# Gate and up products of two ffn stages by Strassen's method

## What is computed

```python
D_FF = 2816
hn = rms_norm_2(h, ffn_norm[l])
gu = hn @ w_gate_up[l]
h = h + (jax.nn.silu(gu[..., :D_FF]) * gu[..., D_FF:]) @ w_down[l]
```

## Time and profile before

| | us |
|---|---|
| median of 3 runs | 3443.02 |
| lowest, highest | 3441.24, 3450.82 |
| profiled execution | 3438.87 |
| its span (first to last instruction) | 3437.1 |
| TensorE matmuls busy (share of the span) | 3069.4 (89%) |
| VectorE busy | 1387.9 (40%) |
| ScalarE busy | 1115.5 (32%) |
| GpSimd busy | 250.7 (7%) |
| first layer: gate and up products | 2310.4 to 2552.2 |
| second layer: gate and up products | 3068.6 to 3310.2 |

### The profile page before, as it was taken

The page is one execution under the profiler, slowest core; times in us unless marked ns, Lnnn a source line. Parts: engine busy times, 40 slices in busy tenths (PEclk is TensorE's granted clock), DMA queues, the critical chain, the costliest instruction groups (busy, mean ns, idle before and its releaser), DMA issues. The chain is left out here.

```text
span 3437.1 us, 44411 instructions
## 1 busy us (share of the span) xinstructions
PE 3069.4 (89%) x17561; PEld 2178.1 (63%) x17561; DVE 1387.9 (40%) x2258; ACT 1115.5 (32%) x1938; POOL 250.7 (7%) x278
## 2 busy tenths in 40 slices
PE   7999999999698878887887698889999998889999
PEld 5777888878533333333333485868888775778887
DVE  6872566663430000000000467553332467553332
ACT  4672666762200000000000435432222336332222
POOL 0000332210000000000000000300000000300000
PEclk9999999999899999999999799999999998999999
DMA  5322222234699999999998520023333320023332
GB/s 135 89 76 80 74 68 68 74 91 136 251 379 429 429 429 429 430 429 429 429 429 357 157 74 13 6 93 98 96 95 104 94 57 1 20 92 96 98 98 92
DMA packets 361295, 612.37 MB, mean 178 GB/s; under 512 B 73952, under 2 KB 308224, under 8 KB 336384
## 3 DMA queue, kind: packets, MB, share of 16 engines
q1 hardware_dynamic: 351152, 598.72, 47.3%
q0 software_dynamic: 9216, 8.42, 0.7%
q10 hardware_dynamic: 720, 2.36, 0.2%
HBM read 605.23 MB, written 23.07 MB: 183 GB/s over the span
## 5 line engine op out<-in xcount | busy, mean ns | idle before, releaser
L268 ACT ACTIVATE f_hi<-f_raw 128x1024 fp32r<-128x1024 f32 x148 | 156.6, 1059 | 516.2 <-PE ff_bk L328 516.0
L1888 PE MATMUL ex_up<-ex_W,ex_XT 128*64 128x512 f32 x1024 | 249.9, 644 | 76.2 <-DMA ex_W<-in_w_expert_up_dram 76.2
L1888 PE MATMUL ex_gp<-ex_W,ex_XT 128*64 128x512 f32 x1024 | 241.3, 625 | 59.2 <-DMA ex_W<-in_w_expert_gate_dram 57.8
L326 PE MATMUL ff_bk<-h_b_hi,f_hi 128*128 128x512 f32 x704 | 276.1, 392 | 2.8 <-DVE h_b_lo L3860 2.8
L327 PE MATMUL ff_bk<-h_b_lo,f_hi 128*128 128x512 f32 x704 | 275.5, 391 | 0.0
L328 PE MATMUL ff_bk<-h_b_hi,f_lo 128*128 128x512 f32 x704 | 275.3, 391 | 0.0
L277 DVE TENSOR_TENSOR f_lo<-f_raw,f_hi 128x1024 fp32r<-128x1024 f32 x148 | 180.5, 1223 | 208.4 <-ACT f_hi L268 208.0
L1917 PE MATMUL ex_yp<-ex_W,ex_hT 128*64 128x512 f32 x1024 | 228.5, 598 | 34.3 <-DMA ex_W<-in_w_expert_down_dram 21.8
L1931 DVE TENSOR_TENSOR ex_hid<-ex_sg,ex_up 128x512 f32<-128x512 f32 x32 | 22.0, 688 | 580.7 <-PE ex_up L1888 580.7
L1888 PEld LDWEIGHTS ex_up<-ex_W,ex_XT 128*64 128x64 f32 x1024 | 89.6, 147 | 235.7 <-issue 235.7
L1888 PEld LDWEIGHTS ex_gp<-ex_W,ex_XT 128*64 128x64 f32 x1024 | 88.0, 144 | 211.3 <-issue 209.5
(11 more groups left out here) (612 smaller groups left out, 6305.8 us busy)
## 6 DMA issues: line engine op xcount, KB each, us to landing
ex_W<-in_w_expert_up_dram SPq DMA_DIRECT2D x64, 2048.0 KB, 37.6
ex_W<-in_w_expert_down_dram SPq DMA_DIRECT2D x64, 2048.0 KB, 38.4
ex_W<-in_w_expert_gate_dram SPq DMA_DIRECT2D x64, 2048.0 KB, 37.6
b_raw<-in_w_in_dram SPq DMA_DIRECT2D x88, 512.0 KB, 3.8
f_raw<-in_w_gate_up_dram SPq DMA_DIRECT2D x88, 512.0 KB, 3.7
f_raw<-in_w_down_dram SPq DMA_DIRECT2D x44, 512.0 KB, 3.5
m_raw<-in_w_in_dram SPq DMA_DIRECT2D x20, 512.0 KB, 4.1
m_early<-in_w_in_dram SPq DMA_DIRECT2D x20, 512.0 KB, 4.0
```

The source lines that it names most:

```text
L268: a.activation(self.hi[n % self.SLOTS][:, to], self.raw[n % self.RAW][:, at], ACT.Copy).then_inc(self.cast, 1)
L326: pe.matmul(out, a[0], b[0], start=first, stop=False)
L1888: ins = pe.matmul(ps[part[e], :], XT[b][:, q, part[e]], row_view(slots[e], KD)[:, q, :], start=(q == 0), stop=(q == KD - 1))
```

## The change

The gate and up products of a block are taken together as one product of a 2 x 2 matrix of halves. The contraction (1024) is halved into features 0 to 511 and 512 to 1023; the outputs are the gate half and the up half; the tokens are halved into 0 to 255 and 256 to 511. Strassen's method (in Winograd's form) makes seven products of half size where there were eight: 7 x 4 x 3 matmuls with 256 columns each, for 2 x 8 x 3 with 512.
- **The combinations of h.** Seven operands `hc[0..6]` (four tiles of 128x256 each, hi and lo). Two are quarters of h, one more is another quarter, four are sums of quarters. `make_sums` makes them from `xs` before they are transposed: three operations for token tiles 0 and 2 on GpSimd (s = 0), three for 1 and 3 on VectorE (s = 1). There are 14 groups of transposes, casts and low parts in place of 8, taken in between the products of block 0.
- **The combinations of weights.** `GateWeights` has nine slots of 128x512 (half a former tile), four raw buffers, and seven operands for each block u: three halves of the raw tiles and four sums, which GpSimd makes (`sum`, i = 3 to 6). ScalarE casts all seven to `hi`, VectorE makes all seven `lo`. A sum is written in the place where its `lo` will stand.
- **Putting together.** A block's results lie in four banks (blocks alternate between banks 0 to 3 and 4 to 7). ScalarE copies the first product (`keep_first`), VectorE makes `join_first` (128x512) and `join` (128x256, 128x512, 128x512), each with an operand in PSUM. Then ScalarE's silu, and on GpSimd the product with the up half (`gate_f`), into `raw_f`.
- **f is split later.** `raw_f` is held in float32; `make_f_hi` and `make_f_lo` stand in the down pass, two for each tile of down weights, in the order `FIRST_DOWN`.

The queues are again in order. VectorE's for pass u: low part 0 of block u + 1, join(u - 1), low parts 1 to 5, join_first(u), low part 6. ScalarE's: casts 0 and 1 of block u + 1, silu(u - 1), keep_first(u), casts 2 to 6. GpSimd's: sums 3 and 4 of block u + 1, gate_f(u - 1), sums 5 and 6. TensorE waits for join(u - 2) before block u.

```diff
+FIRST_DOWN = (3, 4, 5, 6, 7, 8, 9, 0, 1, 2, 10)
+F_ORDER = [2 * r + q for r in FIRST_DOWN for q in range(2)]
...
+class GateWeights:
+
+    SLOTS, RAW, EACH = 9, 4, 7
...
+    def wait_free(self, eng, w):
+
+        if w < self.SLOTS:
+            eng.wait_ge(self.W.used, 7 if w < 4 else 8)
+        else:
+            eng.wait_ge(self.used, w - self.SLOTS + 1)
...
+    def load(self, sp, g):
+
+        if g < self.RAW:
+            sp.wait_ge((None, self.W.split_done, self.W.split_done, self.W.used)[g], (0, 7, 8, 8)[g])
+        else:
+            self.wait_spent(sp, g - self.RAW)
+        dst = self.raw[g % self.RAW][:].rearrange("p (k n) -> p k n", n=P)
+        sp.dma_start(dst, self.tiles[g].rearrange("(k p) n -> p k n", p=P)).then_inc(self.loaded[g % self.RAW], 16)
...
+    def sum(self, p, u, i):
+
+        w = self.EACH * u + i
+        g1, g2, u1, u2 = self.halves(u)
+        raw = lambda j: self.sums[(self.EACH * u + j) % self.SLOTS]
+        self.wait_free(p, w)
+        if i == 3:
+            self.wait_loaded(p, 2 * u)
+            self.wait_loaded(p, 2 * u + 1)
+            p.tensor_tensor(raw(3), u1, u2, ALU.add).then_inc(self.summed, 1)
+        elif i == 4:
+            p.drain()
+            p.tensor_tensor(raw(4), raw(3), g1, ALU.subtract).then_inc(self.summed, 1)
+        elif i == 5:
+            p.drain()
+            p.tensor_tensor(raw(5), g2, raw(4), ALU.subtract).then_inc(self.summed, 1)
+        else:
+            p.tensor_tensor(raw(6), g1, u1, ALU.subtract).then_inc(self.summed, 1)
...
+    def make_lo(self, v, w):
+
+        u, i = divmod(w, self.EACH)
+        hi, lo = self.slot(w)
+        v.wait_ge(self.cast, w - 1)
+        if i in (3, 4):
+            v.wait_ge(self.summed, 4 * u + i - 1)
+        src = self.halves(u)[(0, 1, 3)[i]] if i < 3 else self.sums[w % self.SLOTS]
+        v.tensor_tensor(lo, src, hi.bitcast(F32), ALU.subtract).then_inc(self.split_done, 1)
...
+        def before_group(g):
+            if g < 4:
+                return xs[:, g // 2, (g % 2) * T:(g % 2 + 1) * T]
+            combo, s = g // 2, g % 2
+            if combo == 5:
+                return xs[:, 2 + s, T:]
+            lo = {2: 3 * T, 3: 0, 4: 2 * T, 6: T}[combo]
+            return sums[s][:, lo:lo + T]
...
+        def make_sums(eng, s):
+            x0, x1, out = xs[:, s, :], xs[:, 2 + s, :], sums[s]
+            taken = xs[:, s::2, 0:T]
+            eng.tensor_tensor(out[:, 0:2 * T].rearrange("p (a n) -> p a n", a=2), x1.rearrange("p (a n) -> p a n", a=2), taken, ALU.subtract)
+            eng.drain()
+            eng.tensor_tensor(out[:, 2 * T:3 * T], x1[:, T:], out[:, 0:T], ALU.subtract)
+            eng.drain()
+            eng.tensor_tensor(out[:, 3 * T:], x0[:, T:], out[:, 2 * T:3 * T], ALU.subtract).then_inc(sums_ready[s], 1)
...
-                for m in range(BLOCKS):
-                    for j in range(2):
-                        n = GU + 2 * m + j
-                        W.wait(pe, n)
-                        if m >= 2:
-                            pe.wait_ge((sig_ready, f_ready)[j], m - 1)
-                        for q in range(KD):
-                            ins = mm3(pe, bk[4 + 2 * j + m % 2][:], W.tile(n, q), both(h, q), q == 0, q == KD - 1)
-                        ins.then_inc(W.used, 1)
...
+                def gate_product(u, i):
+                    w = EACH * u + i
+                    bank, col = PLACE[i]
+                    out = bk[4 * (u % 2) + bank][:, col:col + 2 * P]
+                    hi, lo = G.slot(w)
+                    G.wait_split(pe, w)
+                    for q in range(4):
+                        at_q = slice(q * P, (q + 1) * P)
+                        ins = mm3(pe, out, (hi[:, at_q], lo[:, at_q]), both(hc[i], q), q == 0, q == 3)
+                    ins.then_inc(G.used, 1)
+
+                pe.wait_ge(x_added, 4)
+                for i in range(EACH):
+                    if i == 2:
+                        for g in range(4, 8):
+                            turn_middle(g)
+                    elif 3 <= i <= 5:
+                        turn_middle(2 * i + 2)
+                        turn_middle(2 * i + 3)
+                    pe.wait_ge(h_lo, 3 + i if i < 2 else 2 * i + 2)
+                    gate_product(0, i)
+                    if i == 1:
+                        pe.drain().then_inc(W.used, 1)
+                for u in range(1, BLOCKS):
+                    if u >= 2:
+                        pe.wait_ge(joined, u - 1)
+                    for i in range(EACH):
+                        gate_product(u, i)
+
+                pe.wait_ge(joined, BLOCKS - 1)
+                for i, r in enumerate(FIRST_DOWN):
+                    pe.wait_ge(f_lo, 2 * i + 2)
+                    rows(DOWN + i, 0, i, DR - 1, fT, r)
...
+                def gate_silu(u):
+                    a.wait_ge(joined, u + 1)
+                    a.activation(z[u % 2][:, 0:T], z[u % 2][:, 0:T], ACT.Silu).then_inc(sig_ready, 1)
+
+                def keep_first(u):
+                    a.wait_ge(G.used, EACH * u + 4)
+                    if u >= 2:
+                        a.wait_ge(f_ready, u - 1)
+                    a.activation(z[u % 2][:, 6 * P:], bk[4 * (u % 2)][:, 0:2 * P], ACT.Copy).then_inc(first_kept, 1)
+                for u in range(BLOCKS - 1):
+                    for i in range(EACH):
+                        G.make_hi(a, EACH * (u + 1) + i)
+                        if i == 1:
+                            if u >= 1:
+                                gate_silu(u - 1)
+                            keep_first(u)
+                gate_silu(BLOCKS - 2)
+                keep_first(BLOCKS - 1)
+                for i in range(2):
+                    make_f_hi(i)
...
-                def product(m):
-                    v.wait_ge(W.used, GU + 2 * m + 2)
-                    v.wait_ge(sig_ready, m + 1)
-                    v.tensor_tensor(sig[m % 2][:], sig[m % 2][:], bk[6 + m % 2][:], ALU.mult).then_inc(f_ready, 1)
-
-                def product_lo(m):
-                    v.wait_ge(f_hi, m + 1)
-                    v.tensor_tensor(fT[1][:, m, :], sig[m % 2][:], fT[0][:, m, :].bitcast(F32), ALU.subtract).then_inc(f_lo, 1)
-
-                for m in range(BLOCKS):
-                    W.make_lo(v, GU + 2 * m + 2)
-                    if m >= 1:
-                        product_lo(m - 1)
-                    W.make_lo(v, GU + 2 * m + 3)
-                    product(m)
...
+                def join_first(u):
+                    b = bk[4 * (u % 2):4 * (u % 2) + 4]
+                    pairs = lambda x: x.rearrange("p (a n) -> p a n", a=2)
+                    v.wait_ge(G.used, EACH * u + 5)
+                    v.wait_ge(first_kept, u + 1)
+                    one = z[u % 2][:, 6 * P:].rearrange("p (a n) -> p a n", a=1).broadcast_to([P, 2, 2 * P])
+                    v.tensor_tensor(pairs(z[u % 2][:, 0:T]), one, pairs(b[1][:]), ALU.add)
+
+                def join(u):
+                    b = bk[4 * (u % 2):4 * (u % 2) + 4]
+                    pairs = lambda x: x.rearrange("p (a n) -> p a n", a=2)
+                    quarters = z[u % 2][:].rearrange("p (a n) -> p a n", a=4)
+                    v.wait_ge(G.used, EACH * u + 7)
+                    v.drain()
+                    v.tensor_tensor(quarters[:, 2, :], quarters[:, 1, :], b[3][:, 0:2 * P], ALU.add)
+                    v.drain()
+                    one = b[0][:, 2 * P:].rearrange("p (a n) -> p a n", a=1).broadcast_to([P, 2, 2 * P])
+                    v.tensor_tensor(quarters[:, 1::2, :], quarters[:, 1:3, :], one, ALU.add)
+                    v.drain()
+                    v.tensor_tensor(quarters[:, 1:3, :], quarters[:, 1:3, :], pairs(b[2][:]), ALU.add).then_inc(joined, 1)
+
+                def make_f_lo(i):
+                    v.wait_ge(f_hi, i + 1)
+                    v.tensor_tensor(fT[1][:, F_ORDER[i], :], raw_f[:, F_ORDER[i], :], fT[0][:, F_ORDER[i], :].bitcast(F32), ALU.subtract).then_inc(f_lo, 1)
+
+                for u in range(BLOCKS - 1):
+                    for i in range(EACH):
+                        G.make_lo(v, EACH * (u + 1) + i)
+                        if i == 0 and u >= 1:
+                            join(u - 1)
+                        if i == EACH - 2:
+                            join_first(u)
...
+            @block.gpsimd
+            def _(p):
+                def gate_f(u):
+                    p.wait_ge(sig_ready, u + 1)
+                    p.tensor_tensor(raw_f[:, u, :], z[u % 2][:, 0:T], z[u % 2][:, T:], ALU.mult).then_inc(f_ready, 1)
+
+                G.sum(p, 0, 3)
+                G.sum(p, 0, 4)
+                p.wait_ge(xs_ready, 3)
+                make_sums(p, 0)
+                G.sum(p, 0, 5)
+                G.sum(p, 0, 6)
+                for u in range(1, BLOCKS):
+                    G.sum(p, u, 3)
+                    G.sum(p, u, 4)
+                    if u >= 2:
+                        gate_f(u - 2)
+                    G.sum(p, u, 5)
```

(77 more changed lines are left out.)

188 lines of the change are left out of this document (114 added, 74 removed).

## The result

The changed kernel takes 3498.1 us (median of 4 runs, 3493.7 to 3500.9) where the kernel before takes 3442.2 (4 runs beside it): a ratio of 1.0156, 95% interval 1.0135 to 1.0177. It is slower by 1.6%; 3491 was forecast. The profiled execution took 3500.9 us, its span is 3499.1 us against 3437.1, so 62.0 us have to be found.

A forecast was written before the change was run, and what follows sets the result against it. TensorE bounds the kernel before; afterwards VectorE and GpSimd turns make blocks 11.95 us against 10.88. Per stage 0.8 + 0.3 + 22.8 = 23.9 us, 48 for both: 3438.9 becomes 3487, plus 4 for the median, 3491; range 3400 to 3530.

The forecast's parts named there:

- The mechanism and the cycle: Gate and up blocks: VectorE and GpSimd operations on SBUF take turns, PSUM operands exempt; 11.95 us a block.
- The lengths: Operations of 128x512 in the blocks: GpSimd 1.27 us, VectorE low part 0.69, join 0.41 + 0.69 + 0.69.
- The flaw: GpSimd's queue: gate_f waits for the silu, so GpSimd idles during the 2 us join, when it would disturb nobody.
- TensorE idle 2 us per block: In each block TensorE needs 9.9 us, then waits for the join, idle 2 us.
- The start: Start of a gate and up stretch: block 0 ends 0.8 us later, blocks 1 and 2 add 0.3.
- the walk: Hand-traced queue order at the stretch's start: sums of h take turns, product 2 at 2312.6, block 0 ends about 2324.5.
- The end: Stretch's end: last pass saves 2.2 us; 4.7 us from join(20) to the first down product.
- The sum: Both gate and up stages: 23.9 us later per stage, 48 together, giving 3491.
- (d): TensorE's clock falls to its lower level through idle in blocks: 19.8 us per block, some 390 us more; chance 0.03.
- (a): Gate and up blocks: TensorE stays the bound, faster; 3407, or 3393 at 0.114 per matmul; chance 0.20.
- (c): VectorE and GpSimd block each other for whole instructions: 12.9 us per block, 3527; chance with higher holds 0.10.
- (b): In between: GpSimd operations take 1.04 or turns fall better, cycle 10.5 to 11.2, 3436 to 3462; chance 0.17.

The follow-up runs named there:

- Experiment 1: Changed kernel without GpSimd's weight sums from the second block of each stage on; casts and low parts read raw halves instead: 3393.4 us, 0.9871.
- 2: Changed kernel with the last of GpSimd's four weight sums made twice in each block from the second on: 3544.4 us, 1.0288.
- 3: Changed kernel with the weight sums of blocks 1 to 21 and gate_f of blocks 0 to 19 moved to VectorE: 3427.8 us, 0.9952.
- experiment 5: Changed kernel with only sums 5 and 6 on GpSimd, beside the join; sums 3 and 4 and gate_f on VectorE: 3395.8 us, 0.9863.
- experiment 4: Changed kernel with GpSimd making sums 3 to 6 in one run and gate_f(u-2) after them: 3433.8 us, 0.9978.
- 8: Changed kernel with low parts of blocks 1 to 21 made as copies of one operand instead of differences: 3398.3 us, 0.9869.

## Why the prediction was right

- **The mechanism and the cycle: right, and shown.** 11.95 us a block was forecast, 12.01 measured. Experiment 1 takes GpSimd's sums away and the cycle is TensorE's; 2 adds one and the cycle grows by 1.09 us (the hold was put at 1.27 - 0.14 = 1.13); 3 and 5 keep the work and move it, and the cycle falls to 10.20 and 9.52.
- **The lengths: right.** GpSimd's 128x512 operation with two full operands, not in the trace of before and taken as 1.27, is 1.30 us undisturbed. VectorE's low part is 0.68, the join's operations 0.42, 0.69, 0.69.
- **The flaw: right, though I gave it up for a while.** The prediction laid the cost to GpSimd standing idle beside the join until the silu. Before experiment 4 I walked the other order by hand, found 11.8 and expected little; it gave 10.93.
- **TensorE idle 2 us per block: the size was a little off.** Its own time is 84 x 0.1133 = 9.52 us, not 9.9, so it loses 2.5 us of 12.01; nearly half is one gap ahead of a block's first product (the waits put it at up to 1.2 us), the rest is in small waits for low parts (0.3 us at most each) and a slower first matmul behind each. The pace was bounded by 0.118 and 0.114; I took the slower. It changes nothing where VectorE is the bound, but it is why 3393 and not 3407 is what is there to be had (experiments 1, 5, 8).
- **The start: two parts were off and cancel, which is luck.** Block 0 took 25.6 us from its first product to that of block 1 (24.4 in the second layer), not 21. Product 2 began 12.7 us behind the first product where the walk had 9.1, and products 2 to 6 took 12.9 where it had 11.9:
```profile
2312.73 1.11 PE L3794 MATMUL ff_bk<-consts,ff_sums 128*128 128x128 f32 x4 [2.95 <-POOL ff_sums L3719]
...
2319.51 0.58 PE L327 MATMUL ff_bk<-ff_hc,f_hi 128*128 128x256 f32 x1 [1.74 <-DVE ff_hc L4076]
2319.89 0.41 PE L328 MATMUL ff_bk<-ff_hc,f_hi 128*128 128x256 f32 x1
```
```profile
2314.82 1.75 DVE L3644 TENSOR_TENSOR f_lo<-f_raw,f_hi 128x512 fp32r<-128x512 f32 x1
```
  TensorE waits 2.95 us for the first sum of h and again 1.74. The walk let VectorE and GpSimd take turns over the sums of h, but counted the two low parts of weights behind them as undisturbed; they meet GpSimd's sums of weights and take 1.75 us each. The matmuls that follow run 0.21 us apart, with the granted clock at the lower level (1.2 GHz) from 2311.9 to 2325.5, behind the pause. Against these 4.6 us stand 3.1 the other way: blocks 1 and 2 took 9.52 us each at TensorE's pace, 19.0 where 22.1 was said; block 3 took 11.2, and the cycle of 12.0 begins with block 4. So from the first gate to the first down product it is 274.3 and 273.1 us where 273 was said.
- **The end: right.** The last pass took 9.8 us (11.95 - 2.2 = 9.75), and from join(20) to the first down product it was 4.4 (4.7):
```profile
2576.94 0.28 PE L329 MATMUL ff_bk<-ff_hc,f_lo 128*128 128x256 f32 x1
2581.08 0.47 PE L327 MATMUL ff_bk<-f_hi,fT_lo 128*128 128x512 f32 x1 [3.87 <-DVE f_lo L278]
```
- **The sum: 7 us short.** The two stretches with their starts give 49.3 (48 said). The remaining 12.7 us were in no term. Of them, 3.7 are the down passes and the end; 1.7 us in the first layer and 1.6 in the second are a down pass that begins at the slower level behind the 3.87 us pause (granted clock 0.66 from 2581 to 2586, where the kernel before had 1.00 at the start of its down pass). The prediction had placed a pause of 4.7 us there and had named slow matmuls behind idle of 3.9 us in its rival (d), but put nothing for them at this place. The other 9 lie in stages whose work is the same in both kernels. I can't show their cause: among the changed kernel and its nine variants, whose code outside the stretch is the same, the span less the two stretches goes from 2939 to 2952 us, so 9 us there may be no more than what one profiled execution scatters. By the medians the change costs 55.9 us.
- **The rivals.** (a) TensorE as the bound is what the same work gives in another order (experiment 5), not what this order gives. (c), whole-instruction blocking, is refuted by the cycle and by each handover. (b) would have needed shorter GpSimd operations or turns that fall better: the first did not come (1.30 us), and its cycle, 10.93, is what the other order of experiment 4 gives. (d) didn't occur in the blocks: from 2434.7 to 2542.9 the granted clock is 1.00 in spite of a gap in each block; it fell only behind the longer pauses at the start and the end.
